# Expert weights laid out by contiguous runs, and a selection matmul that reads the tokens with a stride of eight

## The reference, cut to what matters

```python
def hier_moe(x, w_group, w_expert, w_gate, w_up, w_down):
    ...                                  # router: group, top 2 of its 8 experts, weights
    def expert_block(args):
        xb, e = args                     # 128 rows of 1024
        h = jax.nn.silu(xb @ w_gate[e]) * (xb @ w_up[e])   # 1024 -> 512
        return h @ w_down[e]                               # 512 -> 1024
    yb = lax.map(expert_block, (rows, block_expert)).reshape(P, d)
    out = jax.ops.segment_sum(yb * row_w[:, None], row_tok, num_segments=T + 1)[:T]
```

## Time and profile before

| what | value |
|---|---|
| time, median of 3 runs | 2484.46 us (2482.36 to 2484.93) |
| time of the profiled execution | 2484.86 us |
| its span, first to last instruction | 2483.1 us |
| mean granted TensorE clock | 0.844 |
| TensorE busy | 2119.0 us, 85% of the span |
| VectorE / ScalarE / GpSimd busy | 27% / 13% / 7% |
| moved by DMA | 574.69 MB in 246122 packets |
| of it expert weights (192 loads of 2 MB) | 402.7 MB |

### The profile page before, as it was taken

How to read it: one execution, slowest core, us unless ns; L and a number is a source line. 1 busy time by engine, 2 the same in 40 slices (tenths; PEclk the granted TensorE clock), 3 DMA queues, 4 the chain that set the end, 5 groups by cost and what they waited for, 6 DMA issues and landing times. The chain is left out here.

```text
span 2483.1 us, 33384 instructions
## 1 busy us (share of the span) xinstructions
PE 2119.0 (85%) x13513; PEld 1427.3 (57%) x13513; DVE 667.5 (27%) x2009; ACT 313.5 (13%) x841; POOL 175.2 (7%) x224
## 2 busy tenths in 40 slices
PE   8999789888877498679878888488889989889997
PEld 7776466556555344366555555244478734448863
DVE  4354321111111315421111111328432112833211
ACT  2122000000000013100000000012322101222100
POOL 0112101000000100000000000100001100000110
PEclk9999867777888697767777777689899999989999
DMA  9333459999999742259999999852144342212420
GB/s 335 125 129 109 128 210 396 395 394 395 394 392 393 288 159 95 85 208 363 395 395 395 395 395 394 302 201 102 38 145 142 142 169 103 101 68 102 169 85 25
DMA packets 246122, 574.69 MB, mean 231 GB/s; under 512 B 13316, under 2 KB 16634, under 8 KB 245534
## 3 DMA queue, kind: packets, MB, share of 16 engines
q1 hardware_dynamic: 242974, 569.46, 62.0%
q0 software_dynamic: 3072, 4.21, 0.5%
HBM read 568.39 MB, written 9.44 MB: 233 GB/s over the span
## 5 line engine op out<-in xcount | busy, mean ns | idle before, releaser
L981 PE MATMUL ps<-ring,arena 128*32 128x256 f32 x3968 | 301.8, 469 | 107.6 <-DMA ring<-in_moe_w_up_dram 55.9
L981 PEld LDWEIGHTS ps<-ring,arena 128*32 128x32 f32 x3968 | 169.9, 135 | 250.5 <-issue 207.6
L2097 PE MATMUL ps<-arena,ring 128*128 128x256 f32 x1408 | 304.4, 379 | 1.6 <-DVE arena L244 1.6
L2097 PEld LDWEIGHTS ps<-arena,ring 128*128 128x128 f32 x1408 | 267.4, 190 | 38.5 <-DVE arena L244 2.3
L959 PEld LDWEIGHTS ps<-arena,h 128*128 128x128 f32 x2112 | 256.4, 202 | 29.5 <-issue 26.4
L959 PE MATMUL ps<-arena,h 128*128 128x32 f32 x2112 | 264.0, 286 | 3.0 <-DVE arena L949 3.0
L1394 PE MATMUL ps<-ring,arena 128*128 128x512 f32 (+1 forms) x576 | 250.9, 595 | 2.4 <-DVE arena L244 1.6
L1021 PE MATMUL ps<-ring,arena 128*32 128x256 f32 x1984 | 212.0, 602 | 38.1 <-issue 37.0
L266 PE MATMUL ps<-ring,arena 128*128 128x512 f32 x544 | 239.0, 602 | 1.6 <-DVE arena L1434 0.8
L1394 PEld LDWEIGHTS ps<-ring,arena 128*128 128x128 f32 x576 | 110.1, 193 | 136.2 <-issue 132.4
L266 PEld LDWEIGHTS ps<-ring,arena 128*128 128x128 f32 x544 | 104.8, 193 | 133.2 <-issue 130.4
(11 more groups left out here) (295 smaller groups left out, 1781.5 us busy)
## 6 DMA issues: line engine op xcount, KB each, us to landing
ring<-in_moe_w_gate_dram SPq DMA_DIRECT2D x62, 2048.0 KB, 19.4
ring<-in_moe_w_up_dram SPq DMA_DIRECT2D x62, 2048.0 KB, 22.4
ring<-in_moe_w_down_dram SPq DMA_DIRECT2D x62, 2048.0 KB, 19.8
ring<-in_w_up_dram SPq DMA_DIRECT2D x22, 2048.0 KB, 7.8
ring<-in_ssm_w_in_dram SPq DMA_DIRECT2D x12, 2048.0 KB, 12.2
ring<-in_w_in_dram SPq DMA_DIRECT2D x10, 2048.0 KB, 11.7
ring<-in_w_down_dram SPq DMA_DIRECT2D x10, 2048.0 KB, 7.8
ring<-in_attn_w_qkv_dram SPq DMA_DIRECT2D x6, 2048.0 KB, 20.2
```

Source lines behind the costliest of these rows:

```text
L981: mm = nc.tensor.matmul(ps[j * CAP:(j + 1) * CAP, 2 + b, 0:256], xg[:, b, k * CAP:(k + 1) * CAP], w[:, k, (j % 2) * 256:(j % 2 + 1) * 256] ...
L2097: mm = nc.tensor.matmul(ps[:, n % 4, 0:SEQ], w[:, k, k4 * P:(k4 + 1) * P], xT_mlp[:, k, :], start=(k == 0), stop=(k == KD - 1))
```

## The change

The rows of a weight matrix are dealt to the partitions in another order. For gate and up, partition p gets the eight rows 8p to 8p + 7, one run of 16 KB. For down, it gets two runs of two rows, 8 KB each (rows 2p and 2p + 1 of each half of 256). The tokens have to be picked in the same order: slice k of the features is now k, k + 8, k + 16 and so on, so the stationary operand of the selection matmul is `h` with a step of eight elements (32 bytes), in place. The hidden values are turned with a step of two elements. The number of instructions on each engine, their order, all waits and the bytes moved stay as they are.

```diff
 class Ring:
     def dst(self, c, shape):
+        if len(shape) == 4:
+            return self.rows4(c).rearrange("p (a k) n -> p a k n", a=2)
         return self.rows8(c, shape[2]) if shape[1] == KD else self.rows4(c, shape[1])
...
         def add_experts(layer):
-                add(cols8(t["moe_w_gate"][layer, e], 0, FF))
-                add(cols8(t["moe_w_up"][layer, e], 0, FF))
-                add(rows4(t["moe_w_down"][layer, e], 0))
+                add(t["moe_w_gate"][layer, e].rearrange("(p k) n -> p k n", p=P))
+                add(t["moe_w_up"][layer, e].rearrange("(p k) n -> p k n", p=P))
+                add(t["moe_w_down"][layer, e].rearrange("(a p k) n -> p a k n", a=2, p=P))
...
             def step_pick(pe, s, v, prev, b, e):
-                        nc.tensor.matmul(ps[:, b, k * CAP:(k + 1) * CAP], h[:, tt, k * P:(k + 1) * P],
+                        nc.tensor.matmul(ps[:, b, k * CAP:(k + 1) * CAP], h[:, tt, k:D:KD],
                                          slots[:, b, tt, 0:CAP], start=(tt == 0), stop=(tt == TT - 1))
...
             def step_turn(pe, s, v, prev, b):
-                    mm = nc.tensor.matmul(ps[:, 4 + b, c2 * 64:(c2 + 1) * 64], hid[64:128, b, c2 * P:(c2 + 1) * P],
+                    mm = nc.tensor.matmul(ps[:, 4 + b, c2 * 64:(c2 + 1) * 64], hid[64:128, b, c2:256:2],
                                           ident[64:128, 64:128], start=True, stop=True)
...
                     def load(e, half, used):
                             if part == 2:
-                                src, dst = w.rearrange("a (k p) n -> p (a k) n", p=P), ring.rows4(c)
+                                src = w.rearrange("e (a p k) n -> p (e a) k n", a=2, p=P)
+                                dst = ring.rows4(c).rearrange("p (a k) n -> p a k n", a=2)
                             else:
-                                src, dst = w.rearrange("a (k p) n -> p (a k) n", p=P), ring.rows8(c)
+                                src, dst = w.rearrange("e (p k) n -> p (e k) n", p=P), ring.rows8(c)
```

More of the change, by code:

```diff
@@ L1087, in _ @@
                     for part, name in enumerate(("moe_w_gate", "moe_w_up", "moe_w_down")):
-                        sp.dma_start(w1[part], t[name][layer, 1].rearrange("(k p) n -> p k n", p=P))\
-                            .then_inc(w1_loaded.sem, 16)
+                        w = t[name][layer, 1]
+                        if part == 2:
+                            src = w.rearrange("(a p k) n -> p a k n", a=2, p=P)
+                            dst = w1[part].rearrange("p (a k) n -> p a k n", a=2)
+                        else:
+                            src, dst = w.rearrange("(p k) n -> p k n", p=P), w1[part]
+                        sp.dma_start(dst, src).then_inc(w1_loaded.sem, 16)
                     def load(e, half, used):
@@ L1122, in _ @@
                                 for part, name in enumerate(("moe_w_gate", "moe_w_up", "moe_w_down")):
-                                    w = t[name][layer, bass.ds(e, 1)].rearrange("a (k p) n -> p (a k) n", p=P)
-                                    dst = ring.rows4(first + part) if part == 2 else ring.rows8(first + part)
-                                    sp.dma_start(dst, w).then_inc(o["loaded"].sem, 16)
+                                    w = t[name][layer, bass.ds(e, 1)]
+                                    if part == 2:
+                                        src = w.rearrange("e (a p k) n -> p (e a) k n", a=2, p=P)
+                                        dst = ring.rows4(first + part).rearrange("p (a k) n -> p a k n", a=2)
+                                    else:
+                                        src, dst = w.rearrange("e (p k) n -> p (e k) n", p=P), ring.rows8(first + part)
+                                    sp.dma_start(dst, src).then_inc(o["loaded"].sem, 16)
                         sp.wait_ge(y_st[0].sem, 16 * (NE // 2) + 16 * (SEQ // CAP - 1) * NE)
```

## The result

The changed kernel takes 2593.51 us (median of 4 runs, 2591.77 to 2595.08) against 2484.69; the ratio is 1.0438, with a 95% interval from 1.042 to 1.0456. The profiled execution has a span of 2589.9 us, 106.8 more than before, and a mean granted clock of 0.812.

A forecast was written before the change was run, and what follows sets the result against it. TensorE, at 13.45 + 3.6 + 0.25 = 17.3 us per expert against the DMA's 15.0, becomes the bound; +50.5, +53.1 and +7.2 make +110.8 on 2484.86, forecast 2595 us. Range 2412 to 2640; the likeliest case's own, 2565 to 2650.

The forecast's parts named there:

- The mechanism: MoE stages: TensorE at 17.3 us per expert becomes the bound, covering the DMA's faster 15.0; chance 0.56.
- The loads: Expert weight loads: 16 KB pieces run at 430 GB/s, so the DMA's pace gains 1.2 us per expert.
- Rival A: Pick's stride is free on TensorE and the DMA's gain shows: 2417 us, 2451 if longer pieces don't help; chance 0.30.
- The stepping load: Pick's 32 loads, step of 32 bytes: 227 ns from one to the next instead of 114, +3.6 us per expert.
- rival B: Pick's stride penalty is a ratio, 1.66, not a time: +2.3 us per expert, 2506 us; chance 0.08.
- what is paid is the jump at each value: Stepping reads, from VectorE's rows: each jump to the next value costs, 1.72 ns per value against 1.04 contiguous.
- The turn: Hidden values' turn, four loads with a step of two per expert: costed at nothing, at most 0.45 us.
- The clock: Falls earlier, inside pick, so destination and turn matmuls run at the low level: +0.25 us per expert.
- Outside the intervals: Second pick of each layer, ahead of the first L1041: +7.2 us in all; everything outside the two stages unchanged.
- The point where TensorE decides: Pick's load spacing above which TensorE paces the stage, not the DMA: 162 ns; about 175 ns leaves the time unchanged.

The follow-up runs named there:

- stride_only: The kernel before with only the pick reading with a step of eight, loads and turn as before, wrong features; 2591.6 us, ratio 1.0446.
- loads_only: The changed kernel with the pick's stride undone (contiguous columns, wrong features), long loads and turn kept; 2419.82 us, ratio 0.9744.
- step2_runs4k: The changed kernel with gate and up in four runs of 4 KB and the pick reading with a step of two; 2442.96 us, ratio 0.9848.
- half_strided: The changed kernel with the pick's step of eight in slices 0 to 3 only, slices 4 to 7 contiguous; 2585.29 us, ratio 1.0409.
- longer_pick: The changed kernel with tokens pre-sorted by ScalarE, so a contiguous pick, and its first four slices picked twice (48 loads); 2572.71 us, ratio 1.0366.
- step16: The changed kernel with the pick reading with a step of sixteen over both halves of h, columns not those wanted; 2576.27 us (one run).
- step4_runs8k: The changed kernel with gate and up in two runs of 8 KB and the pick reading with a step of four; 2592.48 us, ratio 1.0441.

## Why the prediction was right

- **The mechanism.** TensorE became the bound of the MoE stages through the stepping loads, and the gain of the DMA was covered. `stride_only` and `loads_only` show both halves of this.
- **The loads.** 430 GB/s for pieces of 16 KB was the extrapolation, 426 to 431 are measured. Rival A's 2417 us is what `loads_only` gives, 2419.82. For pieces of 4 KB the prediction had 0.6 us per expert; 4.194 MB at 414 GB/s are 10.13 us, so it should have said 0.7, or 39 us instead of 34. `step2_runs4k`, with the down weights in pieces of 8 KB on top (0.1 us per expert more), saves 39.
- **The stepping load.** 227 ns were taken from VectorE's price of 1.72 ns per value; it is 237. Pick grew by 4.0 us instead of 3.6. The step as such was right, and carrying over the time rather than the ratio (rival B) too. The reason wasn't quite: "what is paid is the jump at each value" fails for a step of two, which jumps at each value as well and costs 6.5 ns a load.
- **The turn.** Costed at nothing, rightly: its four loads with a step of two take 0.54 us together at the full clock (`loads_only`, 614.39) and 0.93 at the low level (the change, 623.75); without a step they take 0.52 (before, 634.07) and 0.93 (`stride_only`, 619.21).
- **The clock.** Here two sizes were off and cancelled. Turn and the group before it run wholly at the low level, +0.55 us (0.25 predicted; 1.96 + 0.55 = 2.51 us from 622.79 to 625.30). Gate-and-up, which I took as unchanged, got the full clock back, -1.06 us. Sum of the terms: 4.0 + 0.55 - 1.06 = 3.5 above 13.57 us, thus 17.07; predicted 17.3. Outside the intervals it erred the other way: 11.5 us instead of 7.2 ahead of them, and 2.0 instead of nothing after them. That the forecast of 2595 us is met within 2 us is luck in part; its terms were further off. There is luck in the pace too: kernels with a shorter pick have the same 17.07 us (last section), so the sum describes this pace but doesn't explain it.
- **What the prediction missed** is that the price isn't 32 loads times a difference. "The point where TensorE decides" was put at a load of 162 ns, as if the steps could be halved at half the cost. `half_strided`, whose loads average 174 ns by that count, lasts 2585 us where that sum gave 2485. The clock falls 3.7 us into its pick, and each of the 16 contiguous loads behind that takes 213 instead of 111 ns.

That a stepping load costs the same at either level is shown: in the pick at 615.20 the clock falls after 3.3 us, and the loads start 236 to 239 ns apart (215 after the first) on both sides of the fall. So at the low level the step costs only 24 ns a load (237 against 213). That stepping loads aren't what makes the clock fall is shown by `longer_pick`, where none steps; that it falls for want of matmul columns is an inference.

## What to carry to other kernels

Before an operand of TensorE is read with a step, count the values per 16 bytes of memory: two float32 are nearly free (118 against 111.5 ns for 128 columns), one costs twice the load. Where the load sets the pace, sort once into a spare tile on an idle engine. And price a longer stretch of few matmul columns with the clock it ends at: put what doesn't depend on the clock last in it.

## What was not expected

- Settled, the pace is 17.07 us per expert in five kernels whose picks last 6.95, 7.24, 7.49, 7.63 and 7.64 us from the first load to the first matmul of the next group (`step16`, `half_strided`, `step4_runs8k`, the change, `stride_only`). What is shorter in pick comes back in gate-and-up: 4.33 us in `step16` against 3.65. In all five the granted clock is at the full level for 6.8 us and at the low one for 10.2 us per expert; in the changed kernel it falls at 618.5 and is back at 628.7, where gate-and-up starts at 628.68. The return of the clock, not the sum of the steps, seems to set the pace; what fixes it at this value stays open.
- A step of sixteen values is cheaper than one of eight, 309 against 334 ns a load, about 217 against 237 from one to the next. The line alone doesn't explain it. It wasn't followed up.
- ScalarE pays for the step as well: 4.07 us for two copies of 1024 values a partition, 2.0 ns per value with the fixed part. Its activation over 1024 contiguous values (L318 above) takes 1.24 us, 1.2 ns per value.
